# Seven block products in the down projection of a two-block decoder kernel

## What is computed

```python
D_MODEL = 2048
D_FF = 5632
        h2 = rms_norm_2(x, norm2_w[l])
        x = x + (jax.nn.silu(h2 @ w_ffn_gate[l]) * (h2 @ w_ffn_up[l])) @ w_ffn_down[l]
    return rms_norm_2(x, norm_f_w)
```

## Time and profile before

| | |
|---|---|
| median of 3 runs | 2229.48 us (2229.16 to 2229.59) |
| the profiled execution | 2230.15 us, of it the span of the profile 2228.8 us |
| TensorE busy | 2208.3 us, 99% |
| VectorE busy | 1529.6 us, 69% |
| ScalarE busy | 1216.5 us, 55% |
| `d.p0c01`, `d.p2c01` start | 1684.77 and 2154.89 us from the span's start |

### The profile page before, as it was taken

The page is one execution under the profiler, slowest core; times in us unless marked ns, Lnnn a source line. Parts: engine busy times, 40 slices in busy tenths (PEclk is TensorE's granted clock), DMA queues, the critical chain, the costliest instruction groups (busy, mean ns, idle before and its releaser), DMA issues.

```text
span 2228.8 us, 29092 instructions
## 1 busy us (share of the span) xinstructions
PE 2208.3 (99%) x11376; PEld 1825.2 (82%) x11376; DVE 1529.6 (69%) x2034; ACT 1216.5 (55%) x1682; POOL 115.6 (5%) x101
## 2 busy tenths in 40 slices
PE   9999999999999999999999999999999999999998
PEld 7888888888888887888888888888888888888886
DVE  5687765767765677675755556768887578855885
ACT  5545665645665664464544546556555355543554
POOL 0002210003220121000000000000000000000000
PEclk9999999999999999999999999999999999999999
DMA  7456677655677675444644446776666665665674
GB/s 257 143 176 177 196 195 232 202 189 173 201 212 233 195 209 143 142 133 147 223 161 151 151 151 196 231 213 190 210 234 200 203 197 187 214 229 177 202 243 150
DMA packets 313386, 427.31 MB, mean 192 GB/s; under 512 B 121057, under 2 KB 121217, under 8 KB 313121
## 3 DMA queue, kind: packets, MB, share of 16 engines
q1 hardware_dynamic: 311088, 418.35, 59.3%
q0 software_dynamic: 1584, 6.16, 1.0%
q10 hardware_dynamic: 576, 0.95, 0.1%
HBM read 396.06 MB, written 2.10 MB: 179 GB/s over the span
## 4 chain that ended last, share of the span: by engine, by line
PE 92%; issue 3%; DVE 2%; ACT 1%; DMA 1%; POOL 1%; SPq 0%; DVEq 0%; ACTq 0%; POOLq 0%
PE ACC L1127 19%; PE ACC L1129 19%; PE ACC L1128 19%; PE ACC L988 3%; PE ACC L989 3%; PE ACC L990 3%; PE SCPV L988 3%; PE SCPV L989 3%; PE SCPV L990 3%; PE SCPV L1060 1%; PE ACC L1059 1%; PE SCPV L1058 1%; PE SCPV L1059 1%; PE ACC L1060 1%; PE ACC L1058 1%
## 5 line engine op out<-in xcount | busy, mean ns | idle before, releaser
L2257 DVE TENSOR_TENSOR WL<-W,WH 128x1024 fp32r<-128x1024 f32 x729 | 894.0, 1234 | 399.3 <-ACT WH L1156 165.8
L1156 ACT ACTIVATE WH<-W 128x1024 fp32r<-128x1024 f32 x729 | 744.8, 1049 | 248.7 <-PE ACC L1129 93.6
L1127 PE MATMUL ACC<-WH,XH 128*128 128x512 f32 x1888 | 764.9, 405 | 4.0 <-ACT arena L1156 3.0
L1129 PE MATMUL ACC<-WH,XL 128*128 128x512 f32 x1888 | 737.1, 390 | 0.0
L1128 PE MATMUL ACC<-WL,XH 128*128 128x512 f32 x1888 | 735.4, 389 | 0.0
L1127 PEld LDWEIGHTS ACC<-WH,XH 128*128 128x128 f32 x1888 | 354.8, 188 | 80.9 <-issue 6.0
L1129 PEld LDWEIGHTS ACC<-WH,XL 128*128 128x128 f32 x1888 | 354.3, 188 | 76.5
L1128 PEld LDWEIGHTS ACC<-WL,XH 128*128 128x128 f32 x1888 | 355.2, 188 | 68.9 <-issue 1.2
L1156 ACT ACTIVATE arena<-arena 128x1024 uint16<-128x1024 uint16 (+5 forms) x98 | 87.1, 893 | 68.9 <-DVE arena L1948 26.0
L1156 ACT ACTIVATE arena<-ACC,reciprocal_roots 128x512 f32<-128x512 f32 x86 | 58.6, 687 | 118.5 <-PE ACC L1129 118.0
L988 PE MATMUL ACC<-WH,XH 128*128 128x512 f32 x264 | 103.2, 391 | 0.0
(11 more groups left out here) (378 smaller groups left out, 2657.5 us busy)
## 6 DMA issues: line engine op xcount, KB each, us to landing
W<-in_w_in SPq DMA_DIRECT2D x84, 1024.0 KB, 5.0
W<-in_a_w_in SPq DMA_DIRECT2D x47, 1024.0 KB, 5.4
W<-in_w_ffn_gate SPq DMA_DIRECT2D x44, 1024.0 KB, 5.4
W<-in_w_ffn_up SPq DMA_DIRECT2D x44, 1024.0 KB, 5.2
W<-in_w_ffn_down SPq DMA_DIRECT2D x44, 1024.0 KB, 5.2
W<-in_b_w_in SPq DMA_DIRECT2D x40, 1024.0 KB, 5.2
W<-in_a_w_out SPq DMA_DIRECT2D x16, 1024.0 KB, 5.8
W<-in_b_w_out SPq DMA_DIRECT2D x16, 1024.0 KB, 6.2
```

The lines of the kernel that those rows point to most:

```text
L1127: MM(out, hx, WH[:, k, 0:ch.width], start=q == 0 and k == 0, stop=False)
L1129: ins = MM(out, lx, WH[:, k, 0:ch.width], start=False, stop=last and k == QK - 1)
L1156: return nc.scalar.activation(out, in_, func, **how)
L2257: TT(tiles_of(M.WL[K.pair(n)], ch, half), raw, tiles_of(M.WH[n % 3], ch, half).bitcast(F32), ALU.subtract).then_inc(*did("weights_rest", n ...
```

## The change

The block of two quads that is done with seven products is no longer only in the `d.gu` chunks, but in every chunk of taker `both` too. The chunks `d.p0c2`/`c3` and `d.p1c2`/`c3` become double chunks `d.p0c23` and `d.p1c23`. `d.p2c2` and `d.p2c3` stay. That makes five new blocks. In a down chunk the block is not the last: with 8 quads the row slices come in the order 0, 2, 1, 3 and the block is slice 1 at quads 4 and 5; with 6 quads the block is slice 1 at quads 2 and 3.

The forms are made for each set of tokens, as there is one buffer for them: for part 0, 1 and 2 of gate and up, and for each down projection; six times, before once. They stand in the program two quads ahead of the first block that uses them. Blocks in down chunks have eight steps of their own on VectorE (`joins`, 128x512 each) that add the products into X, and one copy on ScalarE.

```diff
+ORDERS = {"pair": (0, 1, 2, 3), "both": {3: (0, 1, 2), 4: (0, 2, 1, 3)}}
+PLACES = {"pair": 3, "both": {3: 1, 4: 2}}
...
         add(f"d.p{p}c01", one("w_ffn_down_2", 0), "both", quads=2 * n, row0=done * CH, xs="H", fresh=f"h{p}.d")
-        for c in (2, 3):
-            add(f"d.p{p}c{c}", one("w_ffn_down_2", c * CH), "dve", quads=n, row0=done * CH, xs="H")
+        if p < len(FF_PARTS) - 1:
+            add(f"d.p{p}c23", one("w_ffn_down_2", 2 * CH), "both", quads=2 * n, row0=done * CH, xs="H")
+        else:
+            for c in (2, 3):
+                add(f"d.p{p}c{c}", one("w_ffn_down_2", c * CH), "dve", quads=n, row0=done * CH, xs="H")
...
-    def forms():
-        whole, sums = M.NF.rearrange("p (n k w) -> p n k w", n=2, k=QK)[:, 0], M.NF.rearrange("p (n i k w) -> p n i k w", n=2, i=4, k=HK)[:, 1]
+    def forms(b):
+        block, tokens = K.blocks[b], K.blocks[b].tokens
+        xs, ks, room = block.chunk.xs, slice(QK * block.slice, QK * (block.slice + 1)), M.FORM_ROOM[block.room]
...
+    def block_work(b, q, half, t):
+        ch, where = K.blocks[b].chunk, (q - 2 * place_of(K.blocks[b].chunk), half, t)
+        first = not any(other.tokens == K.blocks[b].tokens for other in K.blocks[:b])
+        j = int(ch.name[4:]) if ch.taker == "pair" else None
+        if first and where == (-2, 0, 0):
+            forms(b)
+        if where == (-1, 0, 0):
+            combine(b, 1)
+            combine(b, 2)
+        if where == (-1, 0, 1):
+            combine(b, 3)
+        if where == (0, 0, 0):
+            combine(b, 4)
+            combination_rest(b, 2)
...
+        if where == (0, 1, 0):
+            if j is not None:
+                joined_products(j)
+            else:
+                joins(b, (0, 1, 2))
```

More of the change, by code:

```diff
@@ L150, with order_of, place_of, block_plan @@
 Chunk = namedtuple("Chunk", "name first quads parts width row0 k0 xs fresh taker tiles")
+def order_of(ch):
+    return ORDERS["pair"] if ch.taker == "pair" else ORDERS["both"][ch.quads // 2]
+def place_of(ch):
+    return PLACES["pair"] if ch.taker == "pair" else PLACES["both"][ch.quads // 2]
+Block = namedtuple("Block", "quad chunk tokens source slice room")
+def block_plan(chunks):
+    blocks, part = [], 0
+    for ch in chunks:
+        if ch.taker not in ("pair", "both"):
+            continue
+        if ch.taker == "pair":
+            part = sum(int(ch.name[4:]) >= start for start in FF_STARTS) - 1
+            tokens, source, room = f"gate and up {part}", "x.d", "d"
+        elif ch.xs == "H":
+            tokens, source, room = f"down {part}", f"h{part}.d", "d"
+        else:
+            tokens, source, room = ch.name[0], {"a": "go.a", "b": "go.b", "c": "mx.c"}[ch.name[0]], ch.name[0]
+        place = place_of(ch)
+        blocks.append(Block(ch.first + 2 * place, ch, tokens, source, order_of(ch)[place], room))
+    return blocks
 def weight_plan():
@@ L962, in pe_program @@
     live = []
[L964 to L995, removed]
@@ L996, in pair, with seven_products @@
+    def seven_products(ch, x, visit, ends):
+        b, hi, lo = K.block_at[ch.first + 2 * place_of(ch)], M.hi[ch.xs], M.lo[ch.xs]
+        block = K.blocks[b]
+        g, u = block.quad, block.quad + 1
+        tokens = lambda a, t, k: a[:, QK * x + k:QK * x + k + HK, t * P:(t + 1) * P]
         A11, A12, A22 = [(tokens(hi, t, k), tokens(lo, t, k)) for t, k in ((0, 0), (0, HK), (1, HK))]
-        S1, S2, S3, S4 = [(M.form_hi[:, i], M.form_lo[:, i]) for i in range(4)]
-        place = lambda n, half: (M.WH[n % 3][:, half * HK:(half + 1) * HK, :], M.WL[K.pair(n)][:, half * HK:(half + 1) * HK, :])
@@ L1010, in pair @@
             for half in range(2):
-                pe.wait_ge(*at("turned", ch.fresh, 6 + half))
+                pe.wait_ge(*at("turned", ch.fresh, 2 * x + half))
         pe.wait_ge(*at("weights_rest", g, 0))
-        if j:
-            pe.wait_ge(*at("product_copied", j - 1))
-        product(PV[0][:, :], A11, place(g, 0), first=True, last=True).then_inc(*did("product", j, 1))
+        wait_empty("PV0")
+        product(PV[0][:, :], A11, weights(g, 0), True, True).then_inc(*did("product", b, 1))
@@ L2476, in program @@
         K.n_quads = len(K.chunk_of)
-        K.pair_first = [c.first + 6 for c in K.chunks if c.taker == "pair"]
-        K.pair_of = {n: j for j, n in enumerate(K.pair_first)}
+        K.blocks = block_plan(K.chunks)
+        K.block_at = {block.quad: b for b, block in enumerate(K.blocks)}
+        K.block_of_pair = {int(block.chunk.name[4:]): b for b, block in enumerate(K.blocks) if block.chunk.taker == "pair"}
+        K.gated_after = {K.blocks[b].quad: j for j, b in K.block_of_pair.items()}
         K.pair = lambda n: 2 if n == K.n_quads - 1 else n % 2
```

353 lines of the change are left out of this document (211 added, 142 removed).

## The result

The changed kernel takes 2250.55 us (median of 4 runs, 2249.30 to 2251.98), the kernel before on the same chip 2229.53: a ratio of 1.0095, 95% interval 1.0077 to 1.0112. It is slower by 21.0 us. The forecast was 2246.2, range 2240 to 2251.

A forecast was written before the change was run, and what follows sets the result against it. TensorE, busy 99% of the span, was taken to bound the kernel, provided nothing else makes it wait. Terms -6.8 + 1.8 + 8.6 + 13.1 = +16.7 us on a median of 2229.5 gave 2246, range 2240 to 2251.

The forecast's parts named there:

- likeliest case: Whole kernel: the summed terms hold and the time lands in 2243.5 to 2248 us; chance 0.60.
- What is removed: Five blocks with 6 matmuls fewer each, 30 x 0.2267 us on TensorE: 6.8 us saved, called certain.
- `d.gu4` and `d.gu8`: Forms behind quads with only rests cost the 0.89 us measured in d.gu0, twice: 1.8 us.
- `d.p0c01` and `d.p1c01`: Forms make the block's third product 4.1 us late, 4.3 with a slow restart; 8.6 us in both chunks.
- restart: Slow restart of TensorE after the third product's wait in d.p0c01 and d.p1c01, as in d.gu0: 4.1 becomes 4.3 us.
- `d.p2c01`: Forms at the chunk's start, where VectorE is still behind: block 12.9 us late, 13.1 with restarts; the largest term.
- steps 4 and 5: In d.p2c01, a later transpose makes product 6 wait 2.1 us; then HL makes the next quad wait another 2.2 us.
- The clock as a case: TensorE's clock falls in d.p2c01's last 4.4 us idle: +2 to +4 us, 2248 to 2250; chance 0.18.
- the saving wins: Rival: VectorE is less than 0.9 us late at each set of forms, giving 2227 or 2223 us; faster, chance 0.05.
- Only the forms' own delay counts in `d.p2c01`: Rival: ScalarE's chain and HL keep up in d.p2c01, so 8.6 us instead of 13.1, total 2242; chance 0.10.
- Idle time of VectorE: VectorE's 13.9 of 43.53 us idle in d.p0c01 lies behind the block, and an in-order queue cannot use it.

The follow-up runs named there:

- Run 5: Kernel before plus blocks only in d.p0c23 and d.p1c23, forms four quads ahead (three in d.gu0) instead of two: 2225.60 us, ratio 0.9983 to the kernel before.
- Run 3: Changed kernel plus nine matmuls nobody reads ahead of the third product in the three c01 chunks: 2247.15 us, ratio 1.0084 to the kernel before.
- run 2: Changed kernel with the forms made only once, in d.gu0, and read by every block: 2235.95 us, ratio 1.0033 to the kernel before.
- run 6: Kernel before plus forms made at the change's places in the c01 chunks and thrown away, and again for d.gu4 and d.gu8: 2235.86 us, ratio 1.0029.
- run 1: Changed kernel without the block in d.p2c01, which is plain quads again: 2237.18 us, ratio 1.0039 to the kernel before.
- run 8: As run 7, but the forms of H three quads ahead of their block instead of two: 2235.06 us, ratio 1.0025 to the kernel before.
- run 7: Changed kernel with blocks on the double chunks' last quad, d.p2c01 plain, forms of X four quads ahead (three in d.gu0): 2234.45 us, ratio 1.0022.

## Why the prediction was right, and what it missed

The direction, the places of the waits and their lengths were right. That the number fell into the range owes something to luck. The result is 2.55 us above the likeliest case (2243.5 to 2248) and 0.45 us below the range's upper end; two of the four runs are above it. What reached that far was an allowance for a falling clock in `d.p2c01`, and the clock took its time elsewhere.

- **What is removed** (6.8 us): right. 30 matmuls fewer, 1.45 and 1.19 us in the two chunks without forms, which have no wait.
- **`d.gu4` and `d.gu8`** (0.89 each): right, 0.92 and 0.98, with the wait at the third product. Run 5 adds that this price is one of place: with the forms four quads ahead it is nothing. `d.gu0` had paid it in the kernel before as well.
- **`d.p0c01` and `d.p1c01`** (4.3 each): the step is right, the size is not. The wait was put at 4.1 us and is 4.03 and 4.01, where and for whom the forecast said. The term that was mis-sized is the restart behind it, put at 0.2 us "as in `d.gu0`". It is 2.6 and 1.6 us more, because the granted clock fell, in `d.p0c01` within the wait and in `d.p1c01` 0.3 us behind it. The forecast looked at the clock only in `d.p2c01`, although it put a wait of the same length here. Run 3 shows it: with the wait cut to 2.00 us by matmuls that nobody reads, the chunk has the forecast length to 0.1 us.
- **`d.p2c01`** (13.1, net 11.7): right, net 11.88, and right step by step. Measured from the chunk's first matmul, the third product is released after 22.18 us (forecast 2177.0 - 2154.89 = 22.11), rest 4 ends after 2193.29 - 2164.87 = 28.42 (forecast 28.36), and quad 4 starts after 33.63 (forecast 2188.2 - 2154.89 = 33.3). Two waits came out shorter, 2.94 for 4.4 and 0.28 for 2.1 us. Not because VectorE was sooner: TensorE came later to them, as its matmuls ahead of both ran at the lower clock. So the clock costs nothing in this chunk, as the forecast's paragraph on it allowed for steps 4 and 5. Run 3 agrees: about half as many slow matmuls there (8 in place of 15), and the chunk is as long, 44.57 us.
- **The clock as a case** was given +2 to +4 us and 18%, for `d.p2c01`. The amount, +4, was right, the place wrong. Its rule, in the Trainium skill, "TensorE: Matmul & The Clock Gate", section on HAM oscillation, is that a TensorE which pauses long enough for data runs its next matmuls at half the clock. The trace agrees for the waits of 4 us (0.427 us instead of 0.227, granted clock 0.50), and not for each shorter one (2.29 and 2.00 us). So the case should have been priced for every wait of about the same length in the sum, 4.1 us as well as 4.4, and not for the longest alone.
- **The rivals**: "the saving wins" needed VectorE less than 0.9 us late; it is 2.3 us late in `d.p0c01` even without forms (run 2). "Only the forms' own delay counts in `d.p2c01`" fails: the forms alone cost 4.7 us there (run 6), the block without them 39.91 - 32.71 = 7.2 (run 2), together the 11.9 that were measured. Both terms are needed, though slow matmuls are part of either price, so the match to 0.1 us is no proof. The block ended 13.2 us late (11.88 + 1.36), not 8.6, with waits at product 6 and at quad 4.
- **Idle time of VectorE** (13.9 us in `d.p0c01`) was said to be no help since it lies behind the block. Run 2 corrects this in part: 2.9 us of it lie ahead, as waits for the transpose and for ScalarE, and the forms use them.

Left open: the changed kernel's runs fall into two groups, 2249.3 and 2251.8 us. The number of slow matmuls behind a wait differs between equal waits (twelve and eight in one run, eight and eight in run 1), which would give such steps, but one profile per kernel cannot show it.

## What to carry to other kernels

A saving on the busiest engine is worth its size only where its helper's queue is ahead by more than the helper's new work; look for the first instruction that is due behind it, not for the helper's share of busy time. When such work costs, try its place first: the same forms two quads earlier turned a change of 1.0009 into one of 0.9983. But move it across a pause of the helper; within a stretch that has none, the move wins nothing (run 8). And a wait of several us on TensorE is to be priced twice, once for itself and once for the matmuls behind it, unless these are themselves ahead of another wait.

## What the hardware showed unexpectedly

- A wait of 4.0 us was followed by 12 and 8 matmuls 0.427 us apart, 1.6 to 2.6 us more than at the usual pace. In the `c01` chunks waits of 2.29 and 2.00 us (runs 2 and 3) were followed by none.
- Pauses of the same length are not followed by the same clock. The pause of 2.07 us ahead of `d.gu8` left it at 1.00 in run 7; in run 8 it fell 0.6 us behind the pause, which cost 1.45 us. In `d.p2c01` of run 3 it fell at 2182.7, behind pauses of 3.31, 0.30 and 2.09 us with matmuls between them. The stretches of that kernel around the fall:

```profile
2180.00:2182.00 2.00, 0.01 (x1) 0.02 (x1) 2.00 (x3) 2.00 (x4) 0.00 (x0) 1.00 0.00 0
2182.00:2182.80 0.80, 0.80 (x3) 0.66 (x4) 0.80 (x1) 0.80 (x2) 0.00 (x0) 0.95 0.00 0
2182.80:2186.00 3.20, 3.20 (x9) 2.52 (x8) 2.06 (x3) 1.22 (x3) 0.00 (x0) 0.50 0.53 145
```

  The pause of 2.09 us passed at a clock of 1.00, and it fell while TensorE was already working again. So the length of the last wait does not settle by itself what follows it.
- Adding 18 matmuls that nobody reads made two chunks 4.1 us shorter (run 3).
